# Two-layer hybrid attention trunk on one core: biased planner lines, values taken in by tile pair, and one output block instead of two among the fills

## What is computed

```
h = concat(meta, x)                                   # 1040 rows
layer 0 (even): h @ w_in (1024 x 4096) -> 4 differential-attention heads (two softmaxes
        with ALiBi, w = p0 - lam * p1, RMS norm), 8 stick-breaking heads of width 64,
        each gated by silu, then concat(...) @ w_out (1024 x 1024)
layer 1 (odd):  h @ w_in -> cq (512), ckv (256), k_pe (64), g (1024)
        q  = rms_norm(cq) @ w_uq  (8 heads, 128 + 64 rotary)
        kv = rms_norm(ckv) @ w_ukv (8 heads, 128 keys + 128 values)
        softmax(q k^T / sqrt(192), chunk-causal mask) @ v, gated, then @ w_out
after each layer: h = layer_norm(alpha * h + y)
return h[16:]
```

## Time and profile before

| | |
|---|---|
| median of 3 runs | 1339.86 us (1338.02 to 1341.89) |
| the profiled execution | 1337.81 us, of which 1336.0 us are the span from its first to its last instruction |
| TensorE busy | 96% of the span |
| VectorE, ScalarE, GpSimd busy | 64%, 44%, 35% |
| mean granted TensorE clock | 0.995 |

### The profile page before, as it was taken

How to read it: one execution, slowest core, us unless ns; L and a number is a source line. 1 busy time by engine, 2 the same in 40 slices (tenths; PEclk the granted TensorE clock), 3 DMA queues, 4 the chain that set the end, 5 groups by cost and what they waited for, 6 DMA issues and landing times.

```text
span 1336.0 us, 22119 instructions
## 1 busy us (share of the span) xinstructions
PE 1286.5 (96%) x8228; PEld 1212.8 (91%) x8228; DVE 860.3 (64%) x1943; ACT 582.5 (44%) x1376; POOL 466.5 (35%) x429
## 2 busy tenths in 40 slices
PE   8999999999999999998999999998999999999997
PEld 8999998999899999997788999998998998998886
DVE  5785858586687848669555323654767676776455
ACT  3444546364745526256101012534666475665200
POOL 4323231323225142246533324563323233234531
PEclk9999999999999999998999999999999999999999
DMA  6100010101010011213233311122111121114342
GB/s 228 33 32 32 33 49 16 49 33 48 33 40 30 32 45 52 66 33 131 72 123 126 112 32 63 64 84 83 33 44 44 53 72 33 40 52 145 116 158 79
DMA packets 46346, 88.25 MB, mean 66 GB/s; under 512 B 3984, under 2 KB 28560, under 8 KB 46112
## 3 DMA queue, kind: packets, MB, share of 16 engines
q1 hardware_dynamic: 43792, 78.45, 17.9%
q10 hardware_dynamic: 2448, 8.39, 1.6%
HBM read 66.84 MB, written 19.98 MB: 65 GB/s over the span
## 4 chain that ended last, share of the span: by engine, by line
PE 75%; DVE 11%; ACT 7%; issue 3%; POOL 2%; DMA 1%; SPq 0%; ACTq 0%; DVEq 0%; POOLq 0%
PE bank L2138 37%; PE bank L2296 14%; PE bank L2209 9%; PE bank L2268 7%; PE bank L2231 6%; DVE ring L1906 2%; ACT rtmp L1442 2%; PE bank L2125 1%; DVE pb L1888 1%; ACT pb L1546 1%; DVE stat L1840 1%; DMA wraw<-in_w 1%; PE bank L2252 1%; ACT ring L1562 1%; ACT ring L1558 1%
## 5 line engine op out<-in xcount | busy, mean ns | idle before, releaser
L2138 PE MATMUL bank<-big,wsp 128*128 128x344 f32 (+2 forms) x2880 | 522.7, 327 | 8.8 <-DVE big L1692 2.8
L2138 PEld LDWEIGHTS bank<-big,wsp 128*128 128x128 f32 x2880 | 457.0, 189 | 15.6 <-POOL wsp L1115 4.7
L1114 POOL TENSOR_SCALAR wsp<-wraw 128x1024 fp32r<-128x1024 f32 (+4 forms) x88 | 85.2, 968 | 540.4 <-PE bank L2138 421.0
L1906 DVE TENSOR_TENSOR ring<-bank,ring 128x512 fp32r<-128x512 f32 (+3 forms) x280 | 154.9, 570 | 70.7 <-ACT ring L1558 43.5
L2296 PE MATMUL bank<-big,wsp 128*128 128x512 f32 x800 | 192.0, 398 | 1.8 <-DVE big L1945 1.2
L2296 PEld LDWEIGHTS bank<-big,wsp 128*128 128x128 f32 x800 | 149.4, 189 | 37.1 <-DVE big L1945 1.7
L1115 POOL TENSOR_TENSOR wsp<-wraw,wsp 128x1024 fp32r<-128x1024 f32 (+4 forms) x88 | 178.7, 2030 | 7.3
L2138 PE MATMUL bank<-h1t,wsp 128*128 128x344 f32 (+2 forms) x1080 | 173.2, 321 | 1.5 <-DVE lraw L1753 1.5
L2138 PEld LDWEIGHTS bank<-h1t,wsp 128*128 128x128 f32 x1080 | 169.6, 188 | 3.7 <-DVE lraw L1753 1.8
L1558 ACT ACTIVATE ring<-bank 128x512 fp32r<-128x512 f32 (+1 forms) x200 | 105.8, 555 | 107.8 <-PE bank L2231 75.8
L2231 PE MATMUL bank<-eye,pb 128*128 128x128 f32 x892 | 132.7, 275 | 10.4 <-POOL pb L1311 3.5
(11 more groups left out here) (157 smaller groups left out, 1561.0 us busy)
## 6 DMA issues: line engine op xcount, KB each, us to landing
wraw<-in_w SPq DMA_DIRECT2D x47, 512.0 KB, 3.4
wraw<-y_scratch SPq DMA_DIRECT2D x17, 448.0 KB, 3.8
woraw<-in_wo SPq DMA_DIRECT2D x12, 512.0 KB, 5.5
y_scratch<-ot SPq DMA_DIRECT2D x37, 128.0 KB, 1.7
xres<-in_x SPq DMA_DIRECT2D x8, 512.0 KB, 4.6
h_scratch<-res ACTq DMA_DIRECT2D x8, 512.0 KB, 2.6
gate_scratch<-gtmp SPq DMA_DIRECT2D x8, 512.0 KB, 2.9
gate<-gate_scratch SPq DMA_DIRECT2D x8, 512.0 KB, 3.7
```

The costliest lines, as they stand in the source:

```text
L1114: pool.wait_ge(S["pool_step"], tick(nc.gpsimd.tensor_scalar(hi, raw, 1.0, 1.0, ALU.mult, ALU.mult)))
L1906: V.tensor_tensor(to, bank[T_BANK[t]][from_, 0:w], lo_hi(R[from_, r % NRING, 0, 0:w]), ALU.subtract)\
L2138: ins = mm(dst, wsp[:, SLOT[kind, u], a, k, :], rhs[:, b, k0 + k, c0:c0 + w], start=(k == 0 and a == 0 and b == 0), stop=last)
```

## The change

It has four parts. (1) The value steps are reordered: the meta tile [0] is made first, then the tile pairs in order, and the wait of `product` is per group: a product whose tiles end with the group's last pair waits for that pair's step. (2) `FILLS` of layer 1 holds one block; the second one stands behind the attention phase. (3) In `Lines.run` an engine takes the head whose beginning *plus a bias* is smallest; the biases stand in `YIELD`, one table per layer, by engine and line, from -800 to +1600 ns. Before, `NEAR` was 0 for all engines. (4) Some planned costs are changed: the weights of kind A from 1.9 n + 1000 to 1.77 n + 570 ns, the scan of kind B from 2.4 n to 2.09 n + 55, VectorE's low part of an output weight from 2300 to 1250, and 25 ns more in some products. No computation is added or removed.

```diff
-VALUE_STEPS = [[1, 2], [3, 4], [5, 6], [7, 8], [0]]
+VALUE_STEPS = [[0], [1, 2], [3, 4], [5, 6], [7, 8]]
...
-def values_of(u):
-
-    return ("P", "vn", u - u % 2, len(VALUE_STEPS) - 1)
+def new_values(g, tiles):
+
+    return ("P", "vn", GROUPS[g][2] - GROUPS[g][2] % 2, VALUE_STEPS.index(tiles)) if tiles[-1] == GROUPS[g][4][-1] + 1 else None
...
-FILLS = [O_STEPS[:2], O_STEPS[NB + 1:NB + 1 + 2]]
+FILLS = [O_STEPS[:2], O_STEPS[NB + 1:NB + 1 + 1]]
...
-NEAR = {"pe": 0, "act": 0, "dve": 0, "pool": 0, "sp": 0}
+YIELD = [
+    {("pe", "V"): -100, ("act", "E"): -800, ("act", "P"): 300, ("act", "Q"): -300, ("act", "T"): 300, ("act", "W"):
+     300, ("act", "Y"): 1600, ("dve", "C"): 200, ("dve", "F"): 200, ("dve", "M"): -200, ("dve", "O"): 200, ("dve",
+     "P"): -400, ("dve", "S"): -200, ("dve", "W"): -200, ("dve", "Y"): 100, ("pool", "C"): -400, ("pool", "D"): 200,
+     ("pool", "G"): 100, ("pool", "Q"): 200, ("pool", "V"): 50, ("pool", "W"): -400},
+    {("pe", "V"): 400, ("act", "E"): 200, ("act", "P"): -200, ("act", "Q"): 1600, ("act", "S"): 100, ("act", "T"): 50,
+     ("act", "W"): 300, ("act", "Y"): 400, ("dve", "C"): 100, ("dve", "F"): 300, ("dve", "O"): 1600, ("dve", "P"):
+     -100, ("dve", "S"): 100, ("dve", "T"): 200, ("dve", "W"): -400, ("pool", "D"): -50, ("pool", "G"): 400, ("pool",
+     "O"): -400, ("pool", "Q"): -50, ("pool", "V"): -200, ("pool", "W"): 800},
+]
...
-                        heads.append((at, rank, line))
+                        heads.append((at + self.late.get((engine, line), 0), rank, at, line))
                 if heads:
-                    first = min(heads)[0] + NEAR[engine]
-                    at, rank, line = min((h for h in heads if h[0] <= first), key=lambda h: h[1])
+                    _, _, at, line = min(heads)
...
-                L.put("dve", "C", ("C", t), 1.9 * n_all + 1000, [("act", ("E", t, 1)), emptied(g)], 90)
+                L.put("dve", "C", ("C", t), 1.77 * n_all + 570, [("act", ("E", t, 1)), emptied(g)], 90)
...
-                L.put("dve", "C", ("C", t), 2.4 * n_all, [("act", s), emptied(g)], 90)
+                L.put("dve", "C", ("C", t), 2.09 * n_all + 55, [("act", s), emptied(g)], 90)
...
-            L.put("dve", "W", wo, 2300, [("act", wo)], 90)
+            L.put("dve", "W", wo, 1250, [("act", wo)], 90)
...
-                if k == 0 and g == unit_groups(layer, u)[0]:
-                    if layer:
-                        pe.wait_ge(S["proj_evac"], EVAC_AT[values_of(u)])
-                    else:
-                        pe.wait_ge(S["tr_lo"], T_TURN["VT", layer, u, 2] + 1)
+                if layer:
+                    if new_values(g, turns[k]):
+                        pe.wait_ge(S["proj_evac"], EVAC_AT[new_values(g, turns[k])])
+                elif k == 0 and g == unit_groups(layer, u)[0]:
+                    pe.wait_ge(S["tr_lo"], T_TURN["VT", layer, u, 2] + 1)
```

More of the change, by code:

```diff
@@ L273, with __init__ @@
 OUT_PASSES = {s: ((0, 0), (0, 1)) if s[2] == META_Q else ((0, 0), (0, 1), (1, 0)) for s in O_STEPS}
-FILLS = [O_STEPS[:2], O_STEPS[NB + 1:NB + 1 + 2]]
+FILLS = [O_STEPS[:2], O_STEPS[NB + 1:NB + 1 + 1]]
 WO_OWNER = [["dve" if k in (1,2,) else "pool" for k in range(KD)], ["dve" if k % 3 == 1 else "pool" for k in range(KD)]]
 TABLE_NS = 1283
-NEAR = {"pe": 0, "act": 0, "dve": 0, "pool": 0, "sp": 0}
+YIELD = [
+    {("pe", "V"): -100, ("act", "E"): -800, ("act", "P"): 300, ("act", "Q"): -300, ("act", "T"): 300, ("act", "W"):
+     300, ("act", "Y"): 1600, ("dve", "C"): 200, ("dve", "F"): 200, ("dve", "M"): -200, ("dve", "O"): 200, ("dve",
[4 rows of a table added]
+     -100, ("dve", "S"): 100, ("dve", "T"): 200, ("dve", "W"): -400, ("pool", "D"): -50, ("pool", "G"): 400, ("pool",
+     "O"): -400, ("pool", "Q"): -50, ("pool", "V"): -200, ("pool", "W"): 800},
+]
 RANK = {"pe": "SXTVp", "act": "TSEYQPW", "dve": "PTSMCYFWO", "pool": "CDGQVWO", "sp": "FLO"}
 class Lines:
-    def __init__(self, banks, table):
+    def __init__(self, banks, table, late):
         self.table = table
+        self.late = late
         self.lines, self.ended, self.turns, self.turned = {}, {}, [], {}
@@ L359, in weave @@
 def weave(layer):
-    L = Lines(len(TURN_BANKS[layer]), "exp" if layer else None)
+    L = Lines(len(TURN_BANKS[layer]), "exp" if layer else None, YIELD[layer])
     units = range(HEADS if layer else UNITS)
@@ L441, in weave @@
             turned_v = ("pe", ("VT", layer, u, 2)) if first and not layer else None
-            have_v = ("dve", values_of(u)) if first and layer else None
             full, part = [made(t) for t in GROUP_STEPS[g]], []
@@ L453, in weave @@
             x = ("X", g, k)
-            L.put("pe", "X", x, (1 if tiles == [0] else 2 if kind == "B" else 3) * (0.4545 * cols + 1.5 * len(tiles)),
+            have_v = ("dve", new_values(g, tiles)) if layer and new_values(g, tiles) else None
+            L.put("pe", "X", x, (1 if tiles == [0] else 2 if kind == "B" else 3)
+                  * (0.4545 * cols + 1.5 * len(tiles) + 25 * (tiles[-1] == blocks[-1] + 1)),
                   [have_v, ("dve", ("T", g, k)), ("dve", ("Y", g - 1)) if k == 0 and g > groups[0] else None], 170)
@@ L560, in weave @@
         a, d = {"k0": (820, 960), "q0": (820, 960), "g0": (360, 430), "g1": (360, 430), "rms0": (0, 500),
-                "kn": (360, 430), "qn": (360, 430), "qr": (1720, 3280), "vn": (580, 690) if c < 4 else (750, 480)}.get(kind, (0, 435))
+                "kn": (360, 430), "qn": (360, 430), "qr": (1720, 3280), "vn": (580, 690) if c else (750, 480)}.get(kind, (0, 435))
         if kind not in NO_HI:
```

## The result

The changed kernel takes **1344.3 us** (median of 13 runs, 1343.1 to 1348.3) where the kernel before takes 1340.8 (13 runs of the same comparison). The ratio is 1.0025, 95% interval 1.0019 to 1.0032: 3.4 us slower. The prediction said 1333.8 and "faster"; it was wrong in sign.

The account below looks back on a forecast made before the run. TensorE, busy 1286.5 of 1336.0 us, was taken as the bound, so only its idle time could be won. Values -2.5, fill 0, biases and costs -3.6 sum to -6.1: 1339.86 to 1333.8 us, range 1325 to 1344.

Parts of the forecast that it names:

- One fill instead of two: Layer 1's output fills: taking the second block off the list moves no matmul, 0 us.
- dry tail: End of layer 1's attention: the first block might be used up before the last product, leaving TensorE idle, +1.9 us.
- Biases and planned costs: Engine orders in both layers: gaps made by order close, one new gap opens, together -3.6 us.
- one term of layer 0: Layer 0, near 220 us: TensorE's gap waiting for a copy queued late on VectorE closes, -1.44 us.
- one of layer 1: Layer 1, beside the values of heads 2, 4 and 6: three TensorE gaps of about 1.17 us close.
- a new gap: Place not named: the new order makes gaps of its own, taken as one of mean size, +1.3 us.
- planned costs that fit only a VectorE without a busy GpSimd: Rival, both layers: scans and low parts planned too short, three further collisions, +4.0 us, 1343.9 us; chance 0.13.
- Values: Layer 1, first products of heads 2, 4 and 6: their wait for values can't come last any more, -2.5 us.
- The tail of layer 0: Layer 0, 613 to 636: the half-clock stretch stays; at most 3.4 us is lost in it.
- signs of being wrong: Prediction is wrong if idle time in layer 0 grows or a new stretch at 1.2 GHz appears.
- won by order: Gaps made by engine order, counted as won: 1.44 us in layer 0, 3 x 1.17 in layer 1, together -4.9.

Follow-up runs that it names:

- e9: Kernel before with only one output block instead of two among layer 1's fills; ratio 1.0058, +7.8 us against the kernel before.
- e4: Changed kernel without layer 0's biases, its new planned costs kept there; ratio 1.0100, +13.4 us against the kernel before.
- e5: Changed kernel with layer 0 planned as before except the new cost of kind A; ratio 1.0060, +8.0 us against the kernel before.
- e6: Changed kernel with layer 0 planned as before except the new costs other than kind A's; ratio 1.0040, +5.4 us against the kernel before.
- e12: Changed kernel with two fills and layer 0 as before, but kind A there planned at 2.45 n + 730 ns; ratio 0.9949, -6.8 us against the kernel before.
- e10: Kernel before with only layer 1's table of biases added; ratio 0.9942, -7.8 us against the kernel before.
- e16: Kernel before with only two VectorE biases in layer 1, T 200 and C 100 ns back; ratio 0.9993, -0.9 us against the kernel before.
- e7: Kernel before with only the new value steps, the wait per group and their costs; ratio 1.0024, +3.2 us against the kernel before.
- e11: Kernel before with only the value change, but the meta tile second instead of first; ratio 1.0016, +2.1 us against the kernel before.
- e1: Changed kernel with the second output block put back among layer 1's fills; ratio 0.9998, -0.3 us against the kernel before.
- e3: Changed kernel with the old planned costs in layer 0, its new biases kept there; ratio 1.0040, +5.4 us against the kernel before.
- e2: Changed kernel with layer 0 planned as before (no biases, old costs), one fill; ratio 0.9981, -2.5 us against the kernel before.
- e8: Changed kernel with layer 0 planned as before and two fills in layer 1; ratio 0.9948, -7.0 us against the kernel before.
- e14: Kernel before with only VectorE's biases of layer 1; ratio 0.9969, -4.2 us against the kernel before.
- e15: Kernel before with only ScalarE's biases of layer 1; ratio 0.9958, -5.6 us against the kernel before.

## Why the prediction was wrong, step by step

Three steps failed: the fill at 0 us, the planned costs at nothing, and the values at -2.5 us. Only the biases of layer 1 went the way that was forecast.

**One fill instead of two: "0 us", the step that failed most plainly.** Measured 3.6 to 4.4 us in the changed kernel and 7.8 alone. The argument counted the fills in the order of before (31 used of 48) and took that count for the new order, which wants 60. It named the dry tail, and priced it at a gap of 1.9 and "inside the forecast's own range"; it did come, as 2.38 us and a stretch of 3.4 us at half clock, of which at most half is lost: 2.38 + 1.7 = 4.1. What was not seen at all is that taking a block out of the plan also hides its buffers' release from the plan, which turned GpSimd's queue round in e9.

**Biases and planned costs: "-3.6 us".** The sum has one term of layer 0 (-1.44), one of layer 1 (3 x -1.17) and a new gap (+1.3). Layer 0: the 1.44 us gap did close, and the layer became 5.9 to 6.7 us longer. The failed term is the planned costs, which the sum has at nothing: alone they cost 15.9 us. The biases of layer 0, counted as a gain of 1.44, cost 7.9 us alone, and win 10 only in that they repair what the costs break. The rival "planned costs that fit only a VectorE without a busy GpSimd" was nearest to what the runs show, told with the scans and the low parts. That the new costs harm is measured (e4, e5, e6); that they harm because they are too low is supported by e12 alone. The rival overlooked the largest share, the cost of kind A (54.2 us planned, 72.2 taken in the old order), because the differential weights were never summed. It was held at 0.13 with the reason that a cost 1 us too low matters only where the next item is wanted at once. Three such places are the waits at 127, 201 and 275. They sum to 3.6 us; where the rest of the loss arises no list of waits says, as the idle time of layer 0 is the same as before. That its 1343.9 us came close to the measured 1344.3 is luck: the terms are other ones (it had priced three collisions in both layers; the biases of layer 1 then took back what layer 0 and the tail lost).

Layer 1: the term was -3.5 and measured -7.8 (e10). Right in sign, too small, and by another way: the two biases of VectorE that the step names close the three waits (e16) and bring 0.9 +- 1.2 us; what wins is ScalarE's and VectorE's whole tables. How 5.6 us come from ScalarE's table alone isn't shown; its Q at +1600 is the largest entry, and it wasn't tried alone. The list of gaps behind this step had missed one of 1.10 us before a product at 1060.45, ended by L1940; it changes neither the mean nor the term.

**Values: "-2.5 us, the wait can't come last any more".** The wait went as predicted (in the changed kernel no idle time before a product is ended by L1742 or L1746). The lower bound was "0, if the product then waits equally long for its ring buffer"; the part alone costs 3.2 us. The reordering moved the short step to the front, where six matmuls no longer cover the evacuation of the bank that the next step takes. The prediction looked at who waits for the values, not at whose bank each step needs. That is where e7's new waits come from; it does not explain the time, since e11 closes them and stays 2.1 us above the kernel before. What the step costs is thus measured, and why stays open.

**The tail of layer 0.** Predicted as still there at half clock; it is, in this profile 3.4 us longer, with gaps of 1.74 and 3.64 for 1.87 and 1.18. Beside the loss of layer 0 it is small: 0.4 us at equal work in the changed kernel and 0.4 in e1. The wait for L1177 at that place is 4.97 us in e4 (costs alone), 5.00 in e6, 6.5 in 2 waits in e3 (biases alone), and only 0.9 in e2 and 0.3 in e5: the biases make it, and so do the costs of lines W and B, which weren't separated.

**The terms after the fact.** Layer 1's biases -7.8, values and layer 1's costs on top +0.8 (e8 against e10, within their intervals), one fill +4.4, layer 0 +5.9. They are steps of one path (e10, e8, e2, changed kernel), so that they add up to the measured +3.4 is no check. By the other way through the square, over e1, the fill comes to 3.6 and layer 0 to 6.7: the same within the 1.5 us or so to which each term is good. Two of the prediction's own signs of being wrong came true: the idle time from 80 to 636 is 556.00 - 537.76 = 18.2 us, where it wanted less than 15.8, and a new stretch at 1.2 GHz stands in layer 1. The signs of what the prediction called "won by order" were right in layer 1 and wrong in layer 0, where it had written that it had least to go by.

## What to carry to other kernels

A planned cost is a statement about the chip under load: sum the durations of the whole group in the trace and set them beside the sum that the plan makes, before judging a change of cost. When work is taken off a list that fills gaps, count how much of it the *new* order will want, and look for every buffer whose release the planner knew only through that work. A wait that closes is no gain by itself (e16, e14, e15 and e10 all closed the same three waits of 1.17 us and came out 0.9, 4.2, 5.6 and 7.8 us faster): compare the times at which equal work is done, and over several executions.

## What the runs showed of the hardware

TensorE fell to 1.2 GHz for 3.4 us around single gaps: behind 2.38 us idle at 1253.74 in the changed kernel, at the 5.00 us of e9, and in e14 and e16 behind gaps of 1.45 and 1.13 us; the gaps of 1.76 and 1.59 us at 440 and 520 in the changed kernel have none. Where it falls is not a property of the order alone. Eleven kernels with the same order in layer 0 reach the first latent projection between 735.6 (e16), 735.8 (before) and 740.3 (e9), 740.6 us (e11); the new order reaches it at 741.8 (changed kernel) and 745.0 (e1). e14 has its stretch at 221.7, behind the gap that the earlier trace rows show as 1.44 us, and the kernel before has none there. The clock is only a part of it: e9, e10 and e11 also have a wait of 1.76 us at 291 to 294 that the others lack. A single profile of this kernel is thus no evidence for differences up to 5 us.

A VectorE tensor_scalar on 272 columns took 1.45 us beside a GpSimd tensor_tensor of 1024 columns and 0.36 with GpSimd at rest; the order has a part in which of them meet, and the sum over the 36 differential weights went from 72.2 us to 63.8 (29.1 + 21.6 + 7.4 + 5.7) in the changed kernel's order without any change of the work. That lower sum did not make layer 0 shorter.
